# Moving the loads of two x chunks from SyncE's queue to ScalarE's

## The reference

```python
mod = silu(c) @ w_ada + b_ada;  shift, scale, gate = split(mod, 3)
h = rms_norm(x, norm_g) * (1 + scale) + shift
proj = h @ w_in                     # 3592 columns: u, z_pool, q, k, v, o, z_mlstm, gates
pool_out = causal_pool_mixer(u) * silu(z_pool)       # windows 2, 4, 8, 16
q, k = silu(causal_depthwise_conv(proj[q and k]))    # 4 heads of 128
hm = mlstm_chunkwise(q, k, v, ig, lf)                # chunks of 128 tokens
mlstm_out = normed(hm) * sigmoid(o) * silu(z_mlstm)
x = x + gate * (concat[pool_out, mlstm_out] @ w_out)
return rms_norm(x, final_g)
```

## Time and profile before

| | us |
|---|---|
| three executions, median | 1774.49 |
| the profiled execution | 1773.0 |
| its span, from the first to the last instruction | 1771.2 |
| PE busy | 1724.9 (97%) |
| DVE busy | 1270.3 (72%) |
| ACT busy | 714.0 (40%) |
| POOL busy | 322.7 (18%) |

### The profile page before, as it was taken

One profiled execution on the slowest core, in us unless ns is written; L12 is line 12 of the kernel. 1 busy time (PEld: TensorE's weight loads), 2 busy tenths in 40 slices (PEclk: granted clock), 3 DMA queues, 4 the chain that ended last, 5 costly groups with the idle time before them and its releaser, 6 DMA issues.

```text
span 1771.2 us, 25365 instructions
## 1 busy us (share of the span) xinstructions
PE 1724.9 (97%) x8921; PEld 1472.9 (83%) x8921; DVE 1270.3 (72%) x2591; ACT 714.0 (40%) x1644; POOL 322.7 (18%) x273
## 2 busy tenths in 40 slices
PE   6999989989999999999999999999999999999998
PEld 5988778868898888988889888888889888898886
DVE  7787688656886678765876768766787667776683
ACT  4445243343433534334443434345343353433421
POOL 0023122041120303103030121303022030300300
PEclk9899999999999999999999999999999999999999
DMA  9999964589656985569846796468955698566852
GB/s 336 326 307 337 277 179 175 166 257 271 167 185 195 232 285 129 205 192 277 243 96 234 210 277 189 134 230 232 282 142 195 188 252 271 117 216 198 255 166 83
DMA packets 399698, 385.65 MB, mean 218 GB/s; under 512 B 258300, under 2 KB 292052, under 8 KB 399060
## 3 DMA queue, kind: packets, MB, share of 16 engines
q1 hardware_dynamic: 384340, 361.34, 67.1%
q10 hardware_dynamic: 15232, 22.69, 4.5%
HBM read 321.89 MB, written 62.06 MB: 217 GB/s over the span
## 4 chain that ended last, share of the span: by engine, by line
PE 80%; DVE 7%; DMA 6%; SPq 4%; issue 2%; ACT 2%; POOL 0%; ACTq 0%; POOLq 0%; DVEq 0%
PE ps_acc L723 18%; PE ps_acc L725 18%; PE ps_acc L724 18%; SPq L528 3%; PE ps_num L723 3%; PE ps_num L724 3%; PE ps_num L725 3%; PE ps_kv L723 2%; PE ps_kv L724 2%; PE ps_kv L725 2%; DMA sb_w_split<-w_kept 2%; PE ps_kv L1015 1%; PE ps_num L1009 1%; PE ps_num L1008 1%; PE ps_sco L988 1%
## 5 line engine op out<-in xcount | busy, mean ns | idle before, releaser
L723 PE MATMUL ps_acc<-sb_hT_hi,sb_w_split 128*128 128x512 f32 x1088 | 432.7, 398 | 8.5 <-DMA sb_w_split<-w_kept 3.9
L725 PE MATMUL ps_acc<-sb_hT_hi,sb_w_split 128*128 128x512 f32 x1088 | 424.6, 390 | 0.0
L724 PE MATMUL ps_acc<-sb_hT_lo,sb_w_split 128*128 128x512 f32 x1088 | 423.7, 389 | 0.0
L723 PEld LDWEIGHTS ps_acc<-sb_hT_hi,sb_w_split 128*128 128x128 f32 x1088 | 204.4, 188 | 54.4 <-DMA sb_w_split<-w_kept 6.3
L725 PEld LDWEIGHTS ps_acc<-sb_hT_hi,sb_w_split 128*128 128x128 f32 x1088 | 204.2, 188 | 43.9
L724 PEld LDWEIGHTS ps_acc<-sb_hT_lo,sb_w_split 128*128 128x128 f32 x1088 | 204.6, 188 | 39.7
L1522 POOL TENSOR_TENSOR sb_w_split<-sb_w_raw,sb_w_split 128x512 fp32r<-128x512 f32 x92 | 126.4, 1381 | 559.4 <-ACT sb_w_split L1089 559.1
L1089 ACT ACTIVATE sb_w_split<-sb_w_raw 128x512 fp32r<-128x512 f32 x148 | 91.4, 630 | 86.7 <-DMA sb_w_raw<-s_kept 81.1
L2043 DVE SCALAR_TENSOR_TENSOR sb_acc_cv<-sb_shifted,sb_par,sb_acc_cv 128x512 f32<-128x512 f32 x96 | 75.5, 786 | 60.5 <-ACT sb_acc_cv L1346 58.0
L1839 DVE TENSOR_TENSOR sb_w_split<-sb_w_raw,sb_w_split 128x512 fp32r<-128x512 f32 x56 | 57.6, 1028 | 75.2 <-ACT sb_w_split L1089 75.1
L1533 POOL TENSOR_TENSOR sb_h_rs<-sb_h_var,sb_mhalf 128x4 f32<-128x4 f32 x32 | 33.9, 1059 | 403.7 <-DVE sb_h_var L2143 403.7
(11 more groups left out here) (289 smaller groups left out, 3828.5 us busy)
## 6 DMA issues: line engine op xcount, KB each, us to landing
sb_w_split<-w_kept SPq DMA_DIRECT2D x280, 512.0 KB, 4.6
sb_w_split<-w_kept SPq DMA_DIRECT2D x56, 520.0 KB, 4.3
sb_w_raw<-s_kept SPq DMA_DIRECT2D x112, 256.0 KB, 4.2
sb_w_raw<-w_in SPq DMA_DIRECT2D x84, 256.0 KB, 4.5
sb_x_res<-x SPq DMA_DIRECT2D x34, 512.0 KB, 4.6
w_kept<-sb_w_split SPq DMA_DIRECT2D x32, 512.0 KB, 4.8
out<-sb_qT SPq DMA_DIRECT2D x32, 512.0 KB, 2.9
sb_x_in<-x SPq DMA_DIRECT2D x112, 128.0 KB, 3.9
```

Of the source, the lines that this page charges most:

```text
L723: pe.matmul(dst, st_hi, mv_hi, start=start, stop=False, skip_group_check=resumed)
L724: pe.matmul(dst, st_hi, mv_lo, start=False, stop=False, skip_group_check=resumed)
L725: return pe.matmul(dst, st_lo, mv_hi, start=False, stop=stop, skip_group_check=resumed)
```

## The change

`load_x` is given to ScalarE as well, with the same four transfers to a chunk and the same semaphores, and the calls for chunks 0 and 1 of the next block go from SyncE's order (behind the load of m = 52) into ScalarE's (behind `zo_hold(7)`, ahead of `split_zo` of unit 25). In blocks 1 to 6 this moves eight transfers. Block 0, and chunks 2 and 3 of every block, stay with SyncE.

```diff
@@ late_block, SyncE @@
-                    if m == TILE_UNITS[1] and not last:
-                        sp.wait_ge(zo_full, zo_no(b, 7, 1))
-                        load_x(b + 1, 0)
-                        load_x(b + 1, 1)
@@ one_block, ScalarE @@
+                def load_x(nb, c):
+
+                    act.wait_ge(x_turned, (nb - 1) * NC + c - 1)
+                    tokens = x[0, bass.ds(nb * BLK + c * P, P), :].rearrange("(j r) (k q n) -> r k j q n", r=32, q=4, n=32)
+                    for q in range(4):
+                        dst = x_in[32 * q:32 * q + 32, c % 2, :].rearrange("r (k j n) -> r k j n", k=KT, j=NC)
+                        act.dma_start(dst, tokens[:, :, :, q, :]).then_inc(x_loaded[c % 2], 16)
@@ zo_late, ScalarE @@
                     zo_hold(7, zo_c)
+                    if not last_block:
+                        load_x(b + 1, 0)
+                        load_x(b + 1, 1)
                     for u in range(25, 28):
                         split_zo(b, u)
```

## The result

The changed kernel takes 1828.74 us (median of four runs, 1823.68 to 1830.57) against 1773.28 us of the kernel before beside it. The ratio is 1.0309, 95% interval 1.0288 to 1.033: 55 us slower, where 16 were forecast and 1801 was the upper end. The profiled execution has a span of 1827.2 us, 56.0 more than before.

The account below looks back on a forecast made before the run. TensorE was taken as the bound. A stop of 3.72 us a block, 22.3 over six blocks, less 6.1 gained, gave +16.2 us on 1774.5: 1790.7 us, range 1780 to 1801.

Parts of the forecast that it names:

- The direction: Whole kernel: slower, by 16.2 us; all slower outcomes together were given a chance of 0.88.
- ScalarE's sequencer does run ahead: ScalarE, before unit 25: the first x issue goes out beside the copy of unit 24, at 1443.46 in block 6.
- the whole 6.1 us: SyncE, blocks 1 to 6: without the x issues m = 53 loads three microseconds sooner, winning back 6.1 us.
- The rule for the stop: TensorE before unit 25: issue time plus 2.12 us unit less 5.51 available, with the slow restart 3.72 us a block.
- Nothing later in the block took the loss back: Later stages of each block: no later TensorE wait recovers the 22.3 us lost over six blocks.
- the price of eight issues: ScalarE, ahead of the copies of units 25 to 27: eight x issues take 7.0 us a block.
- both bounds: Eight x issues, from SyncE's rows: 5.8 us from below; from above 7.91 and 8.81, mean 8.2.
- rival B: ScalarE's x issues: full stall of 8.2 to 8.8 us, or later start; 1797.9 to 1801.5 us; chance 0.21.
- the restart: TensorE's first matmul behind the stop before unit 25 is slow, costing 0.11 us a block.
- A shared generator: Descriptor generation, locked by one sequencer at a time: ScalarE's x issues and SyncE's two weight loads delay each other by one issue.

Follow-up runs that it names:

- sp_holds: Changed kernel, but SyncE holds back the load of m = 53 and all behind it until both x chunks have landed; 1810.25 us, ratio 1.0201.
- sp_holds52: Changed kernel, but SyncE holds back the load of m = 52 and all behind it until both x chunks have landed; 1789.07 us, ratio 1.0098.
- warm: Changed kernel with 32 unread matmuls added ahead of TensorE's wait for unit 25 in blocks 1 to 6; 1819.13 us, ratio 1.0271.
- act_half: Changed kernel with only chunk 0 of x on ScalarE ahead of unit 25, chunk 1 on SyncE behind m = 56; 1783.55 us, ratio 1.0046.
- sp_spread: Kernel before, but SyncE issues the eight x transfers one by one behind weight loads m = 52 to 59; 1764.15 us, ratio 0.9952.
- act_behind: Changed kernel with the two x calls moved behind ScalarE's copies of units 25 to 27; 1811.2 us, ratio 1.0205.
- act_rows: Changed kernel, but ScalarE's eight x transfers copy whole token rows, pieces of 1024 f32 instead of 32; 1769.55 us, ratio 0.9969.
- act_room: Changed kernel, but ScalarE issues chunks 0 and 1 of x behind its copies of tile u of those chunks, not ahead of unit 25; 1782.55 us, ratio 1.0056.

## Why the prediction was wrong

*Right.* The direction, and where: the copies of units 25 to 27 wait for the issues, GpSimd and TensorE for them, once a block. ScalarE's sequencer does run ahead (the first issue beside the copy of unit 24). All but one of PE's waits for `w_kept` went, and the stretch from scores to scores is 14.46 to 14.49 us in every block, so the whole 6.1 us came back. The rule for the stop held as well: 11.8 + 2.12 - 5.51 gives 8.4 us a block, measured 49.5 / 6 = 8.25. Nothing later in the block took the loss back.

*The step that failed: the price of eight issues, taken as 7.0 us.* It was 11.8, outside both bounds, and this is 6 x 4.8 = 29 us of the 43 by which the blocks' 59.0 us exceed the forecast of 16.2. Both bounds came from SyncE's queue: the lower from a quiet stretch, the upper from issues on a queue that also carried the weights, in one order. There the load of m = 53 and the key load could not leave before the last x issue; that was the very delay that the change removes. I wrote that they would go out three microseconds sooner and booked that as gain, and did not ask what they would run beside. They now leave in the middle of the x issues and take 2.8 us from them; m = 52 takes 1.9 more (sp_holds, sp_holds52). With both held back the issues take 7.1 us, so the 7.0 was the price of a stretch that the change itself does away with; that the middle of my two bounds meets it so closely is chance. I had given rival B at most 8.8 us for the same reason.

*The term that was mis-sized: the restart, taken as 0.11 us a block.* It was 15.5 us in all, 2.6 a block. The row that I read it from follows an idle of 0.25 us. Behind a stop of 7 to 10 us the granted clock is at 1.2 GHz and product 4 runs on it (warm). With the forecast's 3.7 us of stop some of this would have come already: act_half has it behind four of its six stops, sp_holds52 behind four of its six of 2.6 to 4.2 us. The trace of the kernel before held the warning, at 380.70 us.

With the two sizes put in, the sum of the prediction is 49.5 + 15.5 - 6.1 = 59, against 56.0 in the spans and 55 in the medians.

*A shared generator.* The Trainium skill (Perfetto Trace Analysis, DMA Instruction — HWDGE) has one block of descriptor generation, held by one sequencer at a time. No run here shows that it set the price. In block 4 of the changed kernel SyncE's load of m = 53 goes out while an x issue of ScalarE is stalled, and takes its plain 0.33 us:

```profile
1054.38 3.14 ACTq L1289 DMA_DIRECT2D sb_x_in<-x  x1
1056.85 0.33 SPq L465 DMA_DIRECT2D sb_w_split<-w_kept  x1
```

So the stalled issue on one queue did not hold up the other's, whatever it waited for.

The Trainium skill (DMA: Bandwidth & Descriptors, Issuing engines are not separate DMA queues) says that transfers of all issuers run on the same engines and that a second issuer saves only the time of issue. The runs agree with the first half: ScalarE's issues got shorter when SyncE's loads were held back (11.8 to 7.1 us), and four x issues in a row beside weights cost 5.7 us on SyncE and 6.1 on ScalarE (act_half). The saved time of issue is the 6.1 us, and it was paid for ten times over.

*Still open.* What exactly an issue waits for when it is stalled, the queue's room or the transfer engines' backlog. It was tried only from outside, by what runs beside it. Why sp_spread gains 9.8 us in the medians where its profile shows 6.1 in the six blocks is settled in part. The spans of the two profiled executions differ by 8.8 us, and the one of before was 3.3 us behind when product 4 of block 1 began (401.90 against 398.58), ahead of all that the edit touches. The difference lies within the interval.

## What to carry to other kernels

An issue is not free for the engine behind it. On an engine that computes, count each issue of small pieces at its price under load, and ask what stands behind it and for how long that can wait; two issues fitted into the 3.4 us here, four did not. A queue that waits for slots anyhow (SyncE here) can take the same issues one by one for nothing, and beat both kernels.

When a change lets a load leave sooner, ask what it will then run beside. And a stop of TensorE of several microseconds can cost more than its length (15.5 us on top of 49.5 here): look for the granted clock behind it.

## What was not expected of the hardware

- Issues that carry 1024 pieces of 128 bytes take 0.69 us unhindered and up to 6.0 us (act_behind) beside weight loads; the same 128 KB in 32 pieces take 0.34 to 1.0 us (act_rows).
- A stall is not tied to the small pieces: it falls on whatever is issued next, a 256 KB broadcast (up to 6.8 us in act_room) or a 512 KB weight load (3.45 us in sp_spread).
- A stop of TensorE had a slow stretch behind it, its matmuls 0.43 us apart instead of 0.23. In block 6 of the changed kernel the granted clock was 0.5 from 1499 to 1509 us, some 6 us of it with TensorE at work again. In the kernel before it came behind a stop of 1.95 us; behind one of 3.20 us in sp_holds52 it didn't.
- A stalled issue on ScalarE's queue did not delay SyncE's: a weight load went out in 0.33 us in the middle of an x issue of 3.14 us.
